# Output projections of a decoder trunk: full-precision products against three products of rounded parts

## The reference

```python
def hybrid_mixer(hn, w_in, ..., w_out, rel_bias):
    z = hn @ w_in                      # 256 x 2616
    o_a, o_b, o_c, o_d = gla_mixer(...), pool_mixer(...), dsa_mixer(...), sgu_mixer(...)
    return jnp.concatenate([o_a, o_b, o_c, o_d], axis=-1) @ w_out    # (256x1024) @ (1024x1024)

def cross_attn(hn, mem, norm_mem, wq, wkv, wo):
    ...
    return o @ wo                                                    # (256x256) @ (256x1024)

for i in range(DEPTH):                 # DEPTH = 2
    h = h + hybrid_mixer(rmsnorm(h, norm_mix[i]), ...)
    h = h + cross_attn(rmsnorm(h, norm_xa[i]), ...)
    h = h + (swiglu if i % 2 == 0 else moe_swiglu)(rmsnorm(h, norm_ffn[i]), ...)
return rmsnorm(h, final_norm)
```

## Time and profile before

| | us |
|---|---|
| median of 3 runs | 1511.7 (1511.5 to 1511.97) |
| the profiled execution | 1512.51 |
| its span, first to last instruction | 1510.7 |
| PE busy | 1450.5 (96%) |
| DVE busy | 1086.0 (72%) |
| ACT busy | 914.1 (61%) |
| POOL busy | 51.8 (3%) |

### The profile page before, as it was taken

One profiled execution on the slowest core, in us unless ns is written; L12 is line 12 of the kernel. 1 busy time (PEld: TensorE's weight loads), 2 busy tenths in 40 slices (PEclk: granted clock), 3 DMA queues, 4 the chain that ended last, 5 costly groups with the idle time before them and its releaser, 6 DMA issues.

```text
span 1510.7 us, 19223 instructions
## 1 busy us (share of the span) xinstructions
PE 1450.5 (96%) x7312; PEld 1143.1 (76%) x7312; DVE 1086.0 (72%) x1116; ACT 914.1 (61%) x965; POOL 51.8 (3%) x64
## 2 busy tenths in 40 slices
PE   7999999999999999999999999999999999899997
PEld 5776679999877666788888777777777677677675
DVE  1615255555452526988798799899899898998996
ACT  2222243344322224777777688788887797887885
POOL 0230000000014000000000000000000000000000
PEclk9999999999999999999999999999999999999999
DMA  9522523542553055799899899999999999999991
GB/s 320 182 104 77 203 82 128 208 168 85 189 202 109 29 203 201 261 366 371 305 367 365 332 399 415 409 415 413 412 416 410 415 417 406 419 417 407 413 419 59
DMA packets 120581, 435.04 MB, mean 288 GB/s; under 512 B 5694, under 2 KB 30420, under 8 KB 113364
## 3 DMA queue, kind: packets, MB, share of 16 engines
q1 hardware_dynamic: 120340, 433.83, 74.6%
q0 software_dynamic: 192, 0.53, 0.1%
HBM read 433.28 MB, written 1.05 MB: 288 GB/s over the span
## 4 chain that ended last, share of the span: by engine, by line
PE 66%; DVE 17%; issue 12%; ACT 4%; DMA 0%; SPq 0%; DVEq 0%; ACTq 0%
PE bank L1902 23%; PE bank L1474 12%; DVE ring_lo L1380 12%; PE bank L1451 8%; PE bank L1456 6%; PE bank L1736 4%; PE bank L1928 3%; ACT w_hi L865 2%; PE bank L1848 2%; PE bank L1910 1%; DVE h L1217 1%; PE bank L1440 1%; PE bank L1778 1%; PE bank L1631 1%; PE bank L1430 1%
## 5 line engine op out<-in xcount | busy, mean ns | idle before, releaser
L1380 DVE TENSOR_TENSOR ring_lo<-ring,w_hi 128x2048 fp32r<-128x2048 f32 (+1 forms) x352 | 731.7, 2121 | 74.2 <-ACT w_hi L865 73.5
L865 ACT ACTIVATE w_hi<-ring 128x2048 fp32r<-128x2048 f32 (+1 forms) x352 | 610.3, 1777 | 138.1 <-PE bank L1902 138.0
L1902 PE MATMUL bank<-w_hi,xg 128*128 128x512 f32 x1120 | 408.5, 395 | 5.2 <-DVE ring_lo L1380 4.0
L1902 PE MATMUL bank<-ring_lo,xg 128*128 128x512 f32 x896 | 360.3, 402 | 19.4 <-DVE ring_lo L1380 17.3
L1902 PEld LDWEIGHTS bank<-w_hi,xg 128*128 128x128 f32 x1120 | 211.5, 189 | 51.1 <-DVE ring_lo L1380 4.4
L1902 PEld LDWEIGHTS bank<-ring_lo,xg 128*128 128x128 f32 x896 | 168.4, 188 | 76.1 <-DVE ring_lo L1380 41.6
L1902 PE MATMUL bank<-ring_lo,at_hi 128*128 128x512 f32 x400 | 162.3, 406 | 5.0 <-DVE at_hi L1363 5.0
L1902 PE MATMUL bank<-w_hi,at_hi 128*128 128x512 f32 x400 | 157.5, 394 | 0.5 <-DVE at_lo L1365 0.5
L1160 DVE TENSOR_TENSOR wf_lo<-ring,wf_hi 128x1024 fp32r<-128x1024 f32 x66 | 80.6, 1223 | 60.0 <-ACT wf_hi L743 60.0
L743 ACT ACTIVATE wf_hi<-ring 128x1024 fp32r<-128x1024 f32 x66 | 69.6, 1058 | 70.4 <-PE bank L1474 68.8
L1902 PEld LDWEIGHTS bank<-ring_lo,at_hi 128*128 128x128 f32 x400 | 75.1, 188 | 41.6 <-DVE ring_lo L1380 22.2
(11 more groups left out here) (337 smaller groups left out, 1635.3 us busy)
## 6 DMA issues: line engine op xcount, KB each, us to landing
ring<-in_moe_w SPq DMA_DIRECT2D x168, 2048.0 KB, 11.6
ring<-in_ffn_w SPq DMA_DIRECT2D x18, 1536.0 KB, 6.7
ring<-in_w_in SPq DMA_DIRECT2D x6, 2048.0 KB, 15.2
ring<-in_w_out SPq DMA_DIRECT2D x8, 1024.0 KB, 5.0
ring<-in_ffn_w SPq DMA_DIRECT2D x3, 2048.0 KB, 7.8
ring<-in_w_in SPq DMA_DIRECT2D x4, 1024.0 KB, 15.0
ring<-in_xa_wkv SPq DMA_DIRECT2D x2, 2048.0 KB, 14.8
ring<-in_w_in SPq DMA_DIRECT2D x2, 1184.0 KB, 7.3
```

Source lines behind the costliest of these rows:

```text
L865: act.activation(w_hi[:, i % NB, 0:cols.stop - cols.start], ring[:, slot_of(u), cols], ACT.Copy)\
L1380: dve.tensor_tensor(ring_lo[slot_of(u)][:, cols], ring[:, slot_of(u), cols], w_hi[:, i % NB, 0:cols.stop - cols.start], sub).then_inc(S["l ...
L1902: ins = mm(dst[:, :], st_, mv, start=opens, stop=closes, skip_group_check=small)
```

## The change

Each float32 product of the output projections becomes three float32r products (high x high, high x low, low x high), as in the feed-forward parts. For the operand from the mixer there are now `mix_hi` (in the place of `mixT`) and `mix_lo` (in the upper half of ring slot 5). For the weights, ScalarE writes the rounded part of a unit into the upper half of the unit's own slot (`row_hi`), and the difference goes into the lower half (`row_lo`): GpSimd does it for units 0 and 1 of `w_out`, VectorE for units 2 and 3 and for `wo`.

```diff
@@ names
-        mixT = xnT
+        mix_hi = nc.alloc_sbuf_tensor_at("mix_hi", [P, KT, SEQ], F32R, offset=base, align_bytes=32)
+        mix_lo = ring_lo[U_WQ][:, 2048:4096].rearrange("p (k c) -> p k c", k=KT)
+        xo_hi, xo_lo = mix_hi[:, 0:2, :], mix_hi[:, 2:4, :]
-        oxT = kT
+        ROWS = tuple(U_WOUT + n for n in range(4)) + (U_WO,)
+        # row_hi(n): ring_lo[ROWS[n]][:, 2048:4096], row_lo(n): ring_lo[ROWS[n]][:, 0:2048]
+        # hi_of_rows(layer, n): 1 + 5 * layer + (n + 1), lo_of_rows(layer, n): 3 * layer + (n + 2)
@@ GpSimd, behind the scaling of xa_wkv
+                def rows_split(n):
+                    gp.wait_ge(S["bias_row"], hi_of_rows(layer, n))
+                    gp.tensor_tensor(row_lo(n), ring[:, ROWS[n], 0:2048], row_hi(n), ALU.subtract)\
+                      .then_inc(S["wkv_scaled"], 1)
+                for n in range(2):
+                    rows_split(n)
                 gp.wait_ge(g_ev["bu"], L1)
@@ ScalarE
+                def rows_split(n):
+                    act.wait_ge(arrived[ROWS[n]], (layer * (16 * LAYER_TURNS) + 32))
+                    act.activation(row_hi(n), ring[:, ROWS[n], 0:2048], ACT.Copy).then_inc(S["bias_row"], 1)
                 out_of("k", kT[:, :, :], v3(ps[4], 0, 512, 2))
+                rows_split(0)
                 act.wait_ge(S["kd_ps"], L1)
                 act.activation(kdr, v3(ps[2], 0, 256, 2), ACT.Copy).then_inc(S["kdr_done"], 1)
+                rows_split(1)
                 out_of("bu", bu[:, :, PAD:PAD + SEQ], v3(ps[6], 0, 512, 2))
+                rows_split(2)
                 out_of("uv0", uvg[:, 0, :], ps[7][:, :], ACT.Gelu_apprx_tanh)
+                rows_split(3)
                 out_of("uv1", uvg[:, 1, :], ps[4][:, :], ACT.Gelu_apprx_tanh)
...
-                act.activation(mixT[:, 6:8, :], v3(ps[7], 0, 512, 2), ACT.Copy).then_inc(S["mt_a"], 1)
+                act.activation(mix_hi[:, 6:8, :], v3(ps[7], 0, 512, 2), ACT.Copy).then_inc(S["mt_a"], 1)
+                rows_split(4)
@@ VectorE
                 moments(0)
+                rows_split(2)
+                rows_split(3)
                 dve.wait_ge(S["bias_done"], 1)
                 group("uv1")
...
                 for m in range(2):
-                    i = dve.tensor_scalar(mixT[:, 2 + m, :], ps[5][:, 256 * m:256 * m + 256],
+                    i = dve.tensor_scalar(pw1[:, m, PAD:PAD + SEQ], ps[5][:, 256 * m:256 * m + 256],
                                           pcol[:, R_PB + m:R_PB + m + 1], pcol[:, R_PS + m:R_PS + m + 1], add, mult)
-                i.then_inc(g_ev["y"], 1)
+                link(i)
+                dve.tensor_copy(mix_hi[:, 2:4, :], pw1[:, :, PAD:PAD + SEQ]).then_inc(g_ev["y"], 1)
+                dve.wait_ge(g_ev["y"], 2 * layer + 1)
+                dve.tensor_tensor(mix_lo[:, 2:4, :], pw1[:, :, PAD:PAD + SEQ], mix_hi[:, 2:4, :], sub)\
+                   .then_inc(g_ev["y"], 1)
...
                 dve.wait_ge(S["xo_ps"], L1)
-                dve.tensor_copy(oxT[:, :, :], v3(ps[1], 0, 512, 2)).then_inc(S["xo_done"], 1)
+                dve.tensor_copy(xo_hi, v3(ps[1], 0, 512, 2)).then_inc(S["xo_done"], 1)
+                dve.wait_ge(S["xo_done"], 2 * layer + 1)
+                dve.tensor_tensor(xo_lo, v3(ps[1], 0, 512, 2), xo_hi, sub).then_inc(S["xo_done"], 1)
@@ TensorE
+                def times_rows(bank, xh, xl, n, opens, closes, two_ready=None):
+                    if n < 2:
+                        pe.wait_ge(S["wkv_scaled"], lo_of_rows(layer, n))
+                    wh, wl = v3(row_hi(n), 0, 2048, 2), v3(row_lo(n), 0, 2048, 2)
+                    for half in range(2):
+                        cs = slice(512 * half, 512 * half + 512)
+                        for k in range(2):
+                            mm(ps[bank + half][:, :], xh[:, k, :], wh[:, k, cs], start=opens and k == 0, stop=False)
+                            mm(ps[bank + half][:, :], xh[:, k, :], wl[:, k, cs], start=False, stop=False)
+                    if two_ready is not None:
+                        pe.wait_ge(two_ready, 2 * layer + 2)
+                    for half in range(2):
+                        cs = slice(512 * half, 512 * half + 512)
+                        for k in range(2):
+                            i = mm(ps[bank + half][:, :], xl[:, k, :], wh[:, k, cs], start=False, stop=closes and k == 1)
+                    return i
```

More of the change, by code:

```diff
@@ L407, in ffn_buf, with row_hi, row_lo, hi_of_rows @@
             return bufs[:, (i + NB - FFN_EARLY) % NB, :]
+        ROWS = tuple(U_WOUT + n for n in range(4)) + (U_WO,)
+        def row_hi(n):
+            return ring_lo[ROWS[n]][:, 2048:4096]
+        def row_lo(n):
+            return ring_lo[ROWS[n]][:, 0:2048]
+        def hi_of_rows(layer, n):
+            return 1 + len(ROWS) * layer + (n + 1)
+        def lo_of_rows(layer, n):
+            return 3 * layer + (n + 2)
         def as_piece(w, buf):
@@ L1055, in logits, with rows_split @@
                        .then_inc(S["lg"], 1)
+                def rows_split(n):
+                    dve.wait_ge(S["bias_row"], hi_of_rows(layer, n))
+                    dve.tensor_tensor(row_lo(n), ring[:, ROWS[n], 0:2048], row_hi(n), sub)
                 moments(0)
+                rows_split(2)
+                rows_split(3)
                 dve.wait_ge(S["bias_done"], 1)
@@ L1647, in _ @@
                 pe.wait_ge(arrived[U_WKV], landed[1])
-                pe.wait_ge(S["wkv_scaled"], L1)
+                pe.wait_ge(S["wkv_scaled"], lo_of_rows(layer, 0) - 1)
                 pe.wait_ge(g_ev["uv0"], L1)
@@ L1724, in _ @@
                         transpose_rows(5, oc).then_inc(S["mto_ps"], 1)
-                        pe.wait_ge(S["mt_v"], first)
+                        pe.wait_ge(S["mt_v"], 3 * layer + 1)
                     elif m == 3:
-                        pe.wait_ge(S["mt_a"], L1)
+                        pe.wait_ge(S["mt_v"], 3 * layer + 2)
                     else:
-                        pe.wait_ge(S["mt_v"], second)
+                        pe.wait_ge(S["mt_v"], 3 * layer + 3)
                     s = U_WOUT + i4
                     pe.wait_ge(arrived[s], landed[1])
-                    w = v3(ring[:, s, :], 0, 2048, 2)
                     for t in range(TT):
-                        for k in range(2):
-                            for half in range(2):
-                                i = mm(ps[2 * t + half][:, :], mixT[:, 2 * m + k, P * t:P * t + P],
-                                       w[:, k, 512 * half:512 * half + 512],
-                                       start=i4 == 0 and k == 0, stop=i4 == 3 and k == 1)
+                        i = times_rows(2 * t, mix_hi[:, 2 * m:2 * m + 2, P * t:P * t + P],
+                                       mix_lo[:, 2 * m:2 * m + 2, P * t:P * t + P], i4, i4 == 0, i4 == 3,
+                                       g_ev["y"] if m == 1 else None)
                         if i4 == 3 and t == 0:
@@ L1771, in _ @@
                 keep_busy(7, 2)
-                pe.wait_ge(S["xo_done"], L1)
+                pe.wait_ge(S["xo_done"], 2 * layer + 1)
                 pe.wait_ge(arrived[U_WO], landed[1])
-                w = v3(ring[:, U_WO, :], 0, 2048, 2)
                 for t in range(TT):
-                    for half in range(2):
-                        for k in range(2):
-                            i = mm(ps[4 + 2 * t + half][:, :], oxT[:, k, P * t:P * t + P],
-                                   w[:, k, 512 * half:512 * half + 512], start=k == 0, stop=k == 1)
+                    i = times_rows(4 + 2 * t, xo_hi[:, :, P * t:P * t + P], xo_lo[:, :, P * t:P * t + P], 4, True, True,
+                                   S["xo_done"])
                     if t == 0:
```

12 lines of the change are left out of this document (9 added, 3 removed).

## The result

| | before | after |
|---|---|---|
| median of the runs, us | 1511.7 (1511.5 to 1511.97) | 1500.39 (1499.48 to 1501.13) |
| profiled execution, us | 1512.51 | 1500.89 |
| its span, us | 1510.7 | 1499.1 |

The ratio is 0.9923, with an interval of 0.9911 to 0.9934: 0.77% less. The forecast was 1499.5, so 12.2 us less; 11.3 came, 11.6 between the two profiled executions.

A forecast was written before the change was run, and what follows sets the result against it. TensorE's projections were taken to lie on the path, with 5% of the span at stake. Products saving 13.2 us less 1.0 for the hold gave 12.2 off the median 1511.7: 1499.5, own range 1495 to 1502, wider range 1494.5 to 1504.

The forecast's parts named there:

- Products: Projections with `w_out` and `wo`: float32r products at 0.231 us each save 6.6 us a layer, 13.2 in all.
- The pace of 0.215: Bound for the new products: half a float32 record's 0.430 us each, giving 3.9 us more over 240 products.
- the rule of three quarters: Rejected pricing of the projections: three products cost three quarters of one float32 product, saving 17 us, about 1495.5.
- The hold: Before the projection's first unit TensorE waits for VectorE's cast: 0.5 us a layer, 1.0 in all; bounds 0.3 and 0.8.
- ScalarE's copies: Ten float32r weight copies on ScalarE, 1.91 us each, stand in gaps; none of the four results is late.
- GpSimd and VectorE: Weight subtractions beside the pool part: contention within slack, no cost counted; upper bound 0.3 us a layer.
- The expert stage "as before": From the first expert product to the end, the time should be as before.
- the third rival: Expert stage answers to its new neighbourhood: 0.3% shift is 3 us, 1496.5 or 1502.5; chance 0.07, 0.01 undoing the change.
- Half clock in the new products: Rival, L1781 to L1788 in all ten units: TensorE at 1.2 GHz adds 55.5 us, 1555; chance 0.03.
- Routing: Rival: rounding sends tokens to other experts, changing jobs; off by tens of microseconds either way; chance 0.02.
- VectorE and GpSimd: Rival: the engines hold each other up around L1045, costing 1 to 2 us a layer, 1501.5 to 1503.5; chance 0.10.

The follow-up runs named there:

- four units on GpSimd: Against the kernel after: GpSimd makes all four `w_out` subtractions, VectorE only that of `wo`; 1501.97 us, ratio 0.9942.
- `wo` alone: Against the kernel before: only the projection with `wo` in three products, `w_out` stays float32 and unsplit; 1511.0 us, ratio 0.9992.
- `w_out` alone: Against the kernel after: only the projection with `w_out` in three products, `wo` stays float32 and unsplit; 1504.84 us, ratio 0.9945.
- the splits alone: Against the kernel before: all ten copies and ten subtractions made but unused, products still read float32 weights; 1511.74 us, ratio 1.0002.
- VectorE made all five: Against the kernel after: all five low-part subtractions on VectorE, none on GpSimd; 1500.72 us, ratio 0.9929.

## Why the prediction was right, step by step

**Products.** In the rows above seven of them fill 137.91 to 139.54, 0.233 us each. The price of the earlier trace rows held: 5.22 us came with `w_out` (27.98 to 22.76) for 5.3, 1.29 with `wo` for 1.3. The pace of 0.215 did not come, nor did the rule of three quarters, by which A would have shrunk by some 8 us. Its premise, that a float32 product costs four of the passes of the rounded kind, is not what the two rows show: 0.861 is 3.7 times 0.231. The step from four passes to three quarters was mine: the sentence that I had cited gives no pace for the rounded kind.

**The hold.** 0.5 us a layer was forecast. Between the start of the transposes and the first product lie 137.57 - 136.20 = 1.37 us, before 137.48 - 136.55 = 0.93: 0.44. The experiment that takes the cast away from in front of TensorE won 0.48 and 0.45. VectorE's rows after, that of the earlier trace rows and the one behind it:

```profile
136.06 0.99 DVE L1156 TENSOR_SCALAR pw<-bank,pcol 128x256 f32<-128x256 f32 x2
137.09 0.43 DVE L1159 CAST mix_hi<-pw 128x512 fp32r<-128x512 f32 x1
```

The cast takes 0.43, the lower of the two values that I had bounded it by (worked out from 0.294 as I said there, that value is 0.44).

**ScalarE's copies.** Its timeline after, beside the earlier trace rows:

```profile
103.08 0.60 ACT L661 ACTIVATE bu<-bank 128x512 f32<-128x512 f32 x1 [4.73 <-PE bank L1505]
103.58 1.90 ACT L720 ACTIVATE ring_lo<-ring 128x2048 fp32r<-128x2048 f32 x1
...
109.95 0.60 ACT L661 ACTIVATE uvg<-bank 128x512 f32<-128x512 f32 x1 [3.17 <-PE bank L1510]
```

Every result still waits for TensorE (4.73 us before `bu`, 3.17 before `uvg`), so none is late. `bu` stands 0.36 earlier than in the earlier trace rows, as everything in this profile does.

**GpSimd and VectorE.** Here the forecast of no cost was right, and the picture behind it only half. GpSimd's timeline after:

```profile
98.43 4.51 POOL L588 TENSOR_TENSOR ring_lo<-ring,ring_lo 128x2048 fp32r<-128x2048 f32 x1 [3.97 <-ACT ring_lo L720]
103.76 1.04 POOL L605 TENSOR_TENSOR pw<-bu 128x512 f32<-128x512 f32 x1 [0.81 <-ACT bu L661]
...
110.67 0.73 POOL L601 TENSOR_TENSOR pw<-pw,cst 64x256 f32<-64x256 f32 x1
111.48 2.65 POOL L603 TENSOR_TENSOR bu<-pw,bu 64x256 f32<-64x256 f32 x1
114.21 2.66 POOL L601 TENSOR_TENSOR pw<-pw,cst 64x256 f32<-64x256 f32 x1
116.95 1.75 POOL L603 TENSOR_TENSOR bu<-pw,bu 64x256 f32<-64x256 f32 x1
```

and VectorE's in the same stretch:

```profile
111.26 5.03 DVE L1097 TENSOR_TENSOR ring_lo<-ring,ring_lo 128x2048 fp32r<-128x2048 f32 x2
116.89 1.23 DVE L1082 TENSOR_TENSOR xnT<-bias,score 128x1024 f32<-128x1024 f32 x1 [0.60 <-PE bank L1510]
...
129.02 0.17 DVE L1091 TENSOR_SCALAR st<-st 128x4 f32<-128x4 f32 x1
```

GpSimd's subtraction took 4.51 us (forecast 4.2 to 6.2), and the pool part started in time. Then the two engines take turns, instruction by instruction. The first split starts at 111.26 and, at 2.29, ends at 113.55; GpSimd's step of 0.72, issued at 111.48, ends at 114.13, some 0.6 after that. The second split ends at 116.29, and the next step of GpSimd, issued at 114.21, at 116.87. The last one, issued 0.06 after L1082, ends 0.58 behind it. So the short side pays: three steps of 0.72 lost 1.9, 1.9 and 1.0 us, while two splits together lost 5.03 - 4.48 = 0.55. I had counted VectorE's losses only (up to a step of 0.72 for each split and for L1045) and none of GpSimd's. The pool part ended at 118.70 instead of the 115.1 that I called the worst. And VectorE's next work, L1082, was not late at all: it still waited 0.60 us for TensorE, where I had expected it 0.5 to 1.0 late. The cover of 18 us took the one error, and the other was on the safe side. That no cost came of a picture half wrong was in part luck: the experiment with four units on GpSimd shows what the same taking of turns costs where it falls a little later.

The Trainium skill ("SBUF — State Buffer", section "Who interferes with whom") has this as a lock that is held for a whole instruction, with the second to issue blocked; these rows agree with it to about 0.1 us, and so does the kernel with four units on GpSimd, where L1082 was the second: issued 0.03 us after a step of 1.04, it took 2.09 instead of 1.23. I had cited the rule and worked out only half of what it says, the half in which VectorE is second. For the subtraction on GpSimd, where I had bounded 4.2 to 6.2 us from rows, the Trainium skill had a price ("GPSIMD Engine Reference", section "3.1 Elementwise — side-by-side cycle accounting"): 4.497 us for 2048 columns; the row is 4.51.

**The expert stage "as before".** This is the step that was off, by 0.9 us: 910.9 for 910.0. It lies where the third rival put it, but it is of another kind: it was TensorE's clock, which I had read for the stage as a whole as 1.00 from 900 us on the earlier trace rows, and not at its start. TensorE stands still for 4 us there, after its first 12 products, and waits for the first split of the experts' weights. The windows of the kernel after (length, busy time and count of PE, PEld, DVE, ACT and POOL, granted clock, DMA share, GB/s):

```profile
588.00:591.40 3.40, 3.06 (x12) 2.18 (x12) 2.63 (x11) 3.39 (x5) 0.00 (x0) 1.00 0.00 0
591.40:594.80 3.40, 0.00 (x0) 0.00 (x0) 2.29 (x3) 3.20 (x3) 0.00 (x0) 0.88 0.00 0
594.80:598.20 3.40, 2.99 (x7) 2.42 (x8) 3.40 (x5) 0.00 (x0) 0.00 (x0) 0.50 0.00 0
598.20:601.60 3.40, 3.40 (x11) 2.63 (x11) 2.62 (x2) 0.87 (x1) 0.00 (x0) 0.61 0.14 13
601.60:605.00 3.40, 3.40 (x16) 2.76 (x15) 2.29 (x1) 3.37 (x4) 0.00 (x0) 1.00 0.91 330
```

From 593.9 us, late in the gap, the clock is at 0.50, the level of 1.2 GHz, and stays there to 600.9. The kernel before has the same gap (3.99 us, to 607.72), but its clock falls only behind it, near 608.0, and is back at 611.4. Its timeline:

```profile
607.72 0.57 PE L1902 MATMUL bank<-w_hi,xg 128*128 128x512 f32 x1 [3.99 <-DVE ring_lo L1380]
...
610.65 0.63 PE L1902 MATMUL bank<-ring_lo,xg 128*128 128x512 f32 x1
611.08 0.79 PE L1902 MATMUL bank<-w_hi,xg 128*128 128x512 f32 x2
611.71 0.39 PE L1902 MATMUL bank<-ring_lo,xg 128*128 128x512 f32 x1
```

A product of 0.39 took 0.63 before 611 and 0.39 behind it. In the kernel after it is 0.63 from 595.80 to 600.07. From the first expert product to the first one with `y_hi` and `hotT` it is 606.24 - 588.19 = 18.05 us after and 617.76 - 600.70 = 17.06 before, so the whole 0.9 lies in these first 18 us.

The half clock lasted 3.4 us in the kernel before, with `wo` alone (near 608.3 to 611.7) and with four units on GpSimd (near 596.0 to 599.5), and some 7 us in the six other profiles. Why isn't shown. The six are just those in which VectorE subtracts units 2 and 3 of `w_out`; with one or two profiles a kernel this can be an effect of the change or chance, and no run here separates the two.

**Rivals.** Half clock in the new products: no; they start 0.23 us apart throughout A and B. Routing: the router's stretch is 20.50 us in both kernels and the expert stage differs by 0.9, where another number or kind of jobs would have made tens of microseconds. VectorE and GpSimd: above.

## What to carry to other kernels

Three rounded products for one in float32 are priced by finding products of the same shape and kind elsewhere in the trace; here that was right to 0.1 us a layer. Splits that went into gaps of the engines that make them cost nothing here, with two units on GpSimd or with none; with four they cost 1.3 us a layer, because GpSimd's pool part then lay over work of VectorE that has little slack. So an overlap has to be worked out for both engines. What remained to win was the one place where the consumer waits for the high part: write that first, straight from where the result lies, and make the low part behind it. And judge an edit of a microsecond or two by the stretch that it touches, since the total carries differences that belong to other stretches: the four runs with `w_out` alone lie up to 4.8 us apart, and in the kernel with `wo` alone such differences hid most of the gain.

## What the runs showed of the hardware that I had not expected

The same instructions at the start of layer 1 run at either level of the clock. Three profiles show the same 16 products: without a drop, in the kernel with the splits alone,

```profile
422.26 3.70 PE L1494 MATMUL bank<-xnT,ring 128*128 128x256 f32 x16
```

in the kernel before,

```profile
418.83 3.74 PE L1456 MATMUL bank<-ring,xnT 128*128 128x8 f32 x32
422.43 5.39 PE L1451 MATMUL bank<-xnT,ring 128*128 128x256 f32 x16
```

and with `wo` alone.

```profile
417.54 4.33 PE L1489 MATMUL bank<-ring,xnT 128*128 128x8 f32 x32
421.72 6.47 PE L1484 MATMUL bank<-xnT,ring 128*128 128x256 f32 x16
```

TensorE had no gap there (its last one, 0.98 us, ended over 13 us before the clock fell); ahead of them it ran 32 products of eight columns each. In the kernel before the clock was at 0.50 from some 423.6 to 427.0 us, with `wo` alone from some 420.6 to 427.4, which takes in the end of those 32 (4.33 us for 3.74). So the step from the first kernel to the second is 5.39 - 3.70 = 1.69 us, and the next (6.47 - 5.39) + (4.33 - 3.74) = 1.67. With a mean clock of 1.00, 0.96 and 0.91 over 400 to 440 us, these are the steps of 1.7 us that set the middle apart.

Of the runs without a profile the record has the mean granted clock of the whole execution, but not by stretches. With `w_out` alone it was 0.992 in the three runs of 1504.68 to 1505.1 us and 0.996 in the one of 1500.28. With `wo` alone the fastest of ten, 1507.45, has the highest, 0.996, and of the splits alone the slowest, 1514.05, the lowest, 0.991. So much of the scatter goes with the clock, but not all of it (1500.72 and 1503.76 came with 0.992 and 0.993 where VectorE made all five). Where in the span it fell in those runs isn't on record.

Why one execution meets the drop and another doesn't stays open. All 28 runs of the kernel before that were measured beside the experiments have 0.994 or 0.995, where three of four with `w_out` alone have 0.992; so the edit may shift the odds, but four runs don't settle it.
